# Seven tables of stops instead of one: numbers of their own for each body of a decoder-trunk kernel

## The chip, the cores and the metric

The kernel runs on one core of a Trainium2 chip. Its time is the device time of one execution in microseconds (us). Three runs of the kernel before took 3503.97, 3504.54 and 3508.67 us; the median, 3504.54 us, is the number to compare with.

## The reference, cut to what matters

One layer of a decoder trunk over a sequence of 1024 tokens of width 1024, all in f32: a mixer (latent attention with 4 heads, a gated recurrence, differential attention with 4 heads), a cross-attention over 256 memory rows, and a PEER feed-forward part that picks experts by product keys. A final norm follows.

```
q = (h @ w_q).reshape(b, s, PEER_HEADS, 2, PEER_DQ // 2)
sc = einsum('bshcd,cnd->bshcn', q, keys)
top_s, top_i = lax.top_k(sc, PEER_TOPK)            # 16 of 128, twice for each of 8 heads
cand = top_s[..., 0, :, None] + top_s[..., 1, None, :]
best_s, best_c = lax.top_k(cand, PEER_TOPK)        # 16 pairs for each head
act = gelu(einsum('td,thkd->thk', xt, u[et]))      # 128 experts for each token
y = einsum('thk,thkd->td', gt * act, v[et])
```

Every token has 8 x 16 = 128 experts, and for each it reads a row of u and a row of v, 1024 numbers each. For 128 tokens, one expert's rows are a tile of 128 x 1024 f32, 512 KB.

## The kernel before, in words

The sequence is cut into 8 blocks of 128 tokens. For each block the program has a front part (norms, projections, recurrence, attention, cross-attention, choice of experts: the "pieces" of the list `PIECES`) and an expert part of 128 positions. A position is one expert: GpSimd gathers its u tile and its v tile from memory (`gather_u`, `gather_v`), VectorE multiplies the u tile with the block's activations and sums along the row (L1986), ScalarE makes activations and a diagonal matrix from each coefficient (L1466), and TensorE multiplies the diagonal with the v tile and adds into PSUM (`add_row`, L1212). Of every eight v tiles one goes to VectorE instead (L2007).

The two parts are woven. Body b of the loops (b = 1 to 7; `LOOPS` has one body for each, since the attention of block b reads b + 1 key tiles) does the front part of block b between the 128 positions of block b - 1, and near its end some first pieces of block b + 1 (`next_norm`, `next_0` to `next_4`). Before the first body block 0's front part runs alone, and after the last body the positions of block 7 run alone.

How the two parts are woven is written in three lists of tables, `TENSOR_STOPS`, `VECTOR_STOPS` and `SCALAR_STOPS`, one table for each body. A table gives to each piece a row of stops. An engine that comes to the next step of a piece first does all its positions below the stop (`Pace.to`), and then the step. A step at stop 59 thus stands in the engine's program behind position 58 and ahead of position 59. Several steps with one stop follow each other with no position between them. The code that takes a stop is `Pace.part`, and the order of pieces, steps and positions among themselves is fixed; only where the two lists interleave is free.

What sets the order around it:
- Tiles of u and of v have a ring of 8 slots each (`G_RING`). GpSimd issues alternately the gather of u tile i and of v tile i - 12 (`retrieve`). The first waits until VectorE has used u tile i - 8 (`u_used`), the second until TensorE (or VectorE, for its share) has used v tile i - 20 (`v_used`, `v_added`). GpSimd is one queue in order: if either waits, both streams stop.
- On TensorE and ScalarE the v tile at position p is number p - 13 and the diagonal number p - 10 (`SUM_LAG`, `DIAG_LAG`), so that the engines are to be near the same position at any time.
- Weights come through a ring of 4 slots of two slices (`W_RING`), loaded by SyncE ahead as slots come free (`w_used`). SyncE has no stops. Behind the last `next` weights it waits for VectorE's copy at position 18 of the next body (`x_copied`, L1658) before it goes on.
- VectorE turns the end of the choice of experts into indices: `choose_0` hands the first half (`hand_first_ids`), which GpSimd needs before it gathers for the next block, and behind `choose_1` `hand_ids` hands the rest at the end of the body.

The pieces on which the prediction draws: `mla_0` to `mla_3` and `diff_0` to `diff_3` are the attention (on TensorE the scores L1061 and L1065, the transposes L1047 and the values L1073; on ScalarE the exponentials and the copies into pT, `out_pT`, L1252); `mix_out` and `cross_out` are the products L1127, `cross_q` and `peer_q` the products L979, as are the `next` pieces; `top_0` and `top_1` find 16 of 128 in eight rows each (L1869, L1873, L1875); `choose_0` and `choose_1` do the same for four rows each and then turn the places into numbers (two rounds of L1923, L1926, L1928 each, and small operations between).

## Time and profile before

| | us |
|---|---|
| median of three runs | 3504.54 |
| profiled execution, its own time | 3502.22 |
| span of that execution | 3500.1 |
| TensorE busy in the span | 2942.9 (84%) |
| VectorE busy | 2341.0 (67%) |
| GpSimd busy | 2008.2 (57%) |
| ScalarE busy | 814.6 (23%) |

The span runs from the first to the last instruction. Block 0's front part takes about the first 310 us, the seven bodies follow, and the positions of block 7 take the last 350 us. A row of a view names line, engine, operation and tiles; PE is TensorE, DVE VectorE, ACT ScalarE, POOL GpSimd.

### The profile page before, as it was taken

How to read it: one execution, taken by the hardware profiler on the slowest of the kernel's cores; microseconds unless marked ns; L12 is line 12 of the kernel's file. 1: busy time of each engine (PE TensorE's matmuls, PEld its weight loads, DVE VectorE, ACT ScalarE, POOL GpSimd, SP SyncE). 2: the span in 40 equal slices, each digit the busy share in tenths (PEclk: the TensorE clock that was granted, in tenths of full speed). 3: DMA queues.
4: the chain of work that ended last, by engine and by line, in shares of the span. 5: the costliest groups of instructions: out<-in, count | busy, mean ns of one | idle time of the engine just before them, and what ended most of it. 6: DMA issues, size and time to landing. Idle time of an engine off the chain costs nothing.

```text
span 3500.1 us, 34723 instructions
## 1 busy us (share of the span) xinstructions
PE 2942.9 (84%) x10960; PEld 1660.0 (47%) x10960; DVE 2341.0 (67%) x5884; ACT 814.6 (23%) x1924; POOL 2008.2 (57%) x2085
## 2 busy tenths in 40 slices
PE   7786898888997899888987799888998789976777
PEld 6465355533554355444554445544554445522222
DVE  6229756886578765887477855786648866596554
ACT  3111421133111422133211332114221232211111
POOL 1003765666565664666555655666547655577775
PEclk9897999999999999999999999999999999998999
DMA  7787999999999999999999999999999999999998
GB/s 275 259 299 266 409 409 409 408 409 402 409 402 408 399 405 403 407 409 390 405 409 408 397 351 409 409 408 370 354 409 409 409 346 350 390 404 410 409 409 339
DMA packets 387256, 1346.12 MB, mean 385 GB/s; under 512 B 41793, under 2 KB 44865, under 8 KB 386433
## 3 DMA queue, kind: packets, MB, share of 16 engines
q0 software_dynamic: 294912, 1073.87, 78.0%
q1 hardware_dynamic: 91008, 265.83, 20.1%
q10 hardware_dynamic: 1152, 4.19, 0.3%
q8 instruction: 89, 1.46, 0.2%
q14 instruction: 95, 0.77, 0.1%
HBM read 1334.03 MB, written 35.39 MB: 391 GB/s over the span
## 4 chain that ended last, share of the span: by engine, by line
PE 43%; DMA 25%; DVE 14%; POOL 9%; issue 6%; ACT 3%; SPq 0%; DVEq 0%; ACTq 0%; POOLq 0%
PE ps_sum L1212 19%; DMA rows<-in_peer_u,ids_u 9%; PE ps_p L979 7%; DMA rows<-in_peer_v,ids_v 6%; DMA rows<-in_peer_v,ids_u 5%; POOL rows L802 5%; PE ps_s L1127 5%; POOL rows L792 4%; DVE rows L1986 4%; DMA w_ring<-packed 2%; PE ps_s L1065 2%; PE ps_p L1073 2%; DVE feat_b L1873 1%; PE ps_p L1047 1%; DVE feat_b L1869 1%
## 5 line engine op out<-in xcount | busy, mean ns | idle before, releaser
L1212 PE MATMUL ps_sum<-rows,diag 128*128 128x512 f32 x3584 | 1748.0, 631 | 271.9 <-DMA rows<-in_peer_v,ids_v 129.2
L1986 DVE CUSTOM_DVE_ANT_0 rows<-h_cur,rows 128x1024 f32<-128x1024 f32 x1024 | 1228.1, 1220 | 539.7 <-DMA rows<-in_peer_u,ids_u 527.0
L792 POOL DMA_INDIRECT rows<-in_peer_u,ids_u x1024 | 1005.4, 982 | 720.7 <-issue 498.8
L1212 PEld LDWEIGHTS ps_sum<-rows,diag 128*128 128x128 f32 x3584 | 684.1, 201 | 1166.4 <-issue 1047.8
L802 POOL DMA_INDIRECT rows<-in_peer_v,ids_v x512 | 493.5, 964 | 452.2 <-PE ps_sum L1212 295.6
L802 POOL DMA_INDIRECT rows<-in_peer_v,ids_u x512 | 494.4, 966 | 267.8 <-issue 127.3
L1466 ACT ACTIVATE diag<-ident,acts 128x128 f32<-128x128 f32 x896 | 327.4, 394 | 1057.4 <-PE ps_sum L1212 757.5
L979 PE MATMUL ps_p<-hT,w_ring 128*128 128x128 f32 x2944 | 367.8, 286 | 36.1 <-DMA w_ring<-packed 18.0
L979 PEld LDWEIGHTS ps_p<-hT,w_ring 128*128 128x128 f32 x2944 | 362.0, 202 | 68.6 <-issue 42.3
L1772 DVE CUSTOM_DVE_ANT_0 e<-ps_s,bias_t 128x256 f32<-128x256 f32 (+6 forms) x96 | 74.2, 773 | 177.5 <-PE ps_s L1065 70.6
L2007 DVE SCALAR_TENSOR_TENSOR x_cur<-rows,acts,x_cur 128x1024 f32<-128x1024 f32 x128 | 164.0, 1282 | 13.4 <-DMA rows<-in_peer_v,ids_v 13.4
L1843 DVE TENSOR_TENSOR x_next<-x_next,ps_s 128x512 f32<-128x512 f32 x32 | 21.9, 685 | 189.8 <-PE ps_s L1127 189.8
L1454 ACT ACTIVATE acts<-dots 128x8 f32<-128x8 f32 x128 | 26.6, 207 | 453.2 <-DVE dots L1986 453.0
L1127 PE MATMUL ps_s<-w_ring,hT 128*128 128x512 f32 x256 | 117.7, 606 | 12.7 <-DVE hT L1833 6.8
L1379 ACT ACTIVATE e<-e,small 128x256 f32<-128x256 f32 (+6 forms) x96 | 75.4, 786 | 220.6 <-DVE small L1774 220.2
L979 PE MATMUL ps_p<-pT,w_ring 128*128 128x128 f32 x1024 | 118.6, 276 | 1.2 <-DMA w_ring<-packed 0.6
L979 PEld LDWEIGHTS ps_p<-pT,w_ring 128*128 128x128 f32 x1024 | 116.8, 192 | 5.6 <-issue 3.3
L1127 PE MATMUL ps_s<-w_ring,feat_b 128*128 128x512 f32 x256 | 115.4, 594 | 1.1 <-ACT feat_b L1252 0.7
L1065 PE MATMUL ps_s<-k_diff,feat_a 32*128 32x512 f32 (+2 forms) x192 | 84.2, 545 | 24.9 <-DVE small L1774 24.7
L1873 DVE FIND_INDEX8 feat_b<-feat_b,e 128x8 uint32<-128x128 f32 (+1 forms) x384 | 103.4, 279 | 0.0
L1252 ACT ACTIVATE feat_a<-ps_p 128x512 f32<-128x512 f32 (+2 forms) x48 | 26.0, 541 | 317.5 <-PE ps_p L979 317.4
L1986 DVE DVE_READ_ACCUMULATOR2_ANT dots<- 128x1 f32 x1024 | 84.5, 83 | 0.0
(280 smaller groups left out, 2325.7 us busy)
## 6 DMA issues: line engine op xcount, KB each, us to landing
w_ring<-packed SPq DMA_DIRECT2D x343, 512.0 KB, 7.7
w_ring<-in_wstream SPq DMA_DIRECT2D x65, 512.0 KB, 5.3
packed<-in_wstream SPq DMA_DIRECT2D x49, 512.0 KB, 7.9
rows<-in_peer_u,ids_u POOLq DMA_INDIRECT x1024, 13.3
rows<-in_peer_v,ids_u POOLq DMA_INDIRECT x512, 10.7
rows<-in_peer_v,ids_v POOLq DMA_INDIRECT x512, 15.4
bias_rows<-rows SPq DMA_DIRECT2D x5, 1024.0 KB, 12.8
bias_t<-in_x SPq DMA_DIRECT2D x8, 512.0 KB, 6.2
```

The source lines that it names most:

```text
L792: pool.indirect_dma_start(u_rows[:, j % G_RING, :], None, peer_u, bass.IndirectOffsetOnAxis(ap=ids_u[:, j:j + 1], axis=0)).then_inc(u_land ...
L802: pool.indirect_dma_start(v_rows[:, j % G_RING, :], None, peer_v, bass.IndirectOffsetOnAxis(ap=ids[:, j:j + 1], axis=0)).then_inc(v_landed ...
L979: ins = pe.matmul(dst, w[:, k, :], lhs[:, kt, :], start=(kt == 0), stop=(kt == KT - 1))
L1065: ins = pe.matmul(ps_s[:, c0:c1], q_diff[r:r + DK, half // 4, :], k_diff[r:r + DK, half // 4, c0:c1], start=True, stop=True)
L1127: pe.matmul(ps_s[:, n * 512:(n + 1) * 512], lhs[:, kt, :], w, start=(kt == 0), stop=(kt == KT - 1)).then_inc(w_used, 1)
L1212: ins = pe.matmul(ps_sum[:, c * 512:(c + 1) * 512], diag[:, n % 4, :], v_rows[:, j % G_RING, c * 512:(c + 1) * 512], start=(n == 0), stop= ...
L1379: act.activation(buf[:, 0:keys_n], buf[:, 0:keys_n], ACT.Exp, bias=small[:, 32 + n:33 + n], accum_out=small[:, 48 + n:49 + n]).then_inc(s_ ...
L1466: act.activation(diag[:, n % 4, :], ident[:, :], ACT.Copy, scale=coef[:, j:j + 1]).then_inc(diag_made, 1)
L1772: run(dve.tensor_tensor_reduce(buf[:, 0:keys_n], ps_s[:, 0:keys_n], bias[:, 0:keys_n], 1.0, -3.0e38, ALU.add, ALU.max, small[:, 16 + n:17 ...
L1873: dve.max_index(i[:, first:first + 8], v[:, first:first + 8], s).then_inc(top_step, 1)
L1986: dve.tensor_tensor_reduce(row, h_cur[:, :], row, 1.0, 0.0, ALU.mult, ALU.add, dots[:, p:p + 1]).then_inc(u_used, 1)
L2007: dve.scalar_tensor_tensor(x_cur[:, :], v_rows[:, j % G_RING, :], coef[:, j:j + 1], x_cur[:, :], ALU.mult, ALU.add)\
```

## The change

All numbers of the three lists are replaced. Before, the seven tables of each list are the same (the last lacks the `next` pieces). After, each body has its own. Nothing else in the program changes: the same instructions, in the same order within each piece, the same buffers, semaphores and transfers. A part of the diff, for the pieces named below (TensorE's body 5 and 7, VectorE's bodies 1, 5 and 7, ScalarE's body 7; a body's number counts from 1):

```diff
 TENSOR_STOPS, body 5
-"mla_0": (29, 30, 31), ... "diff_2": (45, 47, 48, 49), "diff_3": (49, 49, 51, 51), "join": (54, 56), "mix_out": (56, 56, 58, 58, 58),
+"mla_0": (29, 31, 32), ... "diff_2": (45, 47, 52, 52), "diff_3": (52, 52, 56, 56), "join": (56, 59), "mix_out": (59, 59, 60, 60, 60),
-"next_2": (112, 121, 121, 121, 121), "next_3": (121, 121, 124, 126, 126), "next_4": (126, 128, 128)
+"next_2": (108, 120, 120, 120, 120), "next_3": (120, 120, 120, 120, 120), "next_4": (120, 120, 120)
 TENSOR_STOPS, body 7
-"diff_2": (45, 47, 48, 49), "diff_3": (49, 49, 51, 51), "join": (54, 56), "mix_out": (56, 56, 58, 58, 58),
-"norm_cross": (59, 62), "cross_q": (62, 62, 62, 67, 67),
+"diff_2": (46, 51, 51, 52), "diff_3": (52, 52, 56, 56), "join": (56, 59), "mix_out": (59, 59, 59, 59, 59),
+"norm_cross": (59, 61), "cross_q": (61, 61, 61, 61, 61),
 VECTOR_STOPS, body 1
-"choose_0": (104, 105, 105, 105, 106, 108, 108, 108, 108, 111, 111), "top_1": (113, 113, 113, 113, 114, 117),
-"choose_1": (120, 120, 124, 125, 126, 126, 126, 128, 128, 128, 128)
+"choose_0": (107, 107, 107, 107, 107, 115, 115, 115, 115, 115, 115), "top_1": (115, 115, 115, 115, 123, 128),
+"choose_1": (128, 128, 128, 128, 128, 128, 128, 128, 128, 128, 128)
 VECTOR_STOPS, body 5
+"choose_0": (100, 100, 100, 100, 100, 104, 104, 104, 104, 121, 121), "top_1": (121, 121, 121, 121, 121, 121),
+"choose_1": (121, 121, 122, 123, 123, 123, 123, 123, 123, 123, 123)
 VECTOR_STOPS, body 7
-"top_0": (93, 94, 94, 94, 97, 99)
+"top_0": (95, 95, 95, 95, 95, 95), "choose_0": (95, 95, 95, 95, 104, 104, 104, 104, 104, 104, 104)
 SCALAR_STOPS, body 7
-"diff_0": (34, 38, 42), "diff_1": (42, 42, 42), "diff_2": (47, 47, 48), "diff_3": (48, 51, 53)
+"diff_0": (33, 38, 42), "diff_1": (42, 42, 42), "diff_2": (49, 49, 50), "diff_3": (50, 53, 53)
```

In words, for the rest: TensorE's attention runs from stop 29 (28 in body 3, 30 in body 6) to stop 51 in all bodies before; after, it ends at 52, 50, 52, 51, 56, 52 and 56 in bodies 1 to 7. VectorE's `top` and `choose` steps stand at fewer, larger stops in all bodies: `choose_1` wholly at 128 in body 1 and at 127 in body 2; in body 3 the last two steps of `choose_0`, all of `top_1` and seven steps of `choose_1` at 114; in body 4 the same with four steps of `choose_1`; in body 6 `top_1` at 109 and `choose_1` at 126. ScalarE's third stops of `diff_0` to `diff_3`, ahead of the copies into pT, are 42, 42, 48, 53 before in every body, and 41, 41, 50, 53 in body 5, 42, 42, 49, 49 in body 6 and 42, 42, 50, 53 in body 7 after. TensorE's stops ahead of the transposes that these copies follow are 40, 43, 48, 51 before, and 42, 45, 52, 56 in body 5, 41, 43, 48, 52 in body 6 and 40, 43, 51, 56 in body 7 after. TensorE's ten tiles of `next_2` to `next_4` stand at 116 in body 3 and at 120 in body 5.

## Rows read from the trace of the kernel before

**Rows 1.** The page: busy time of the engines, GB/s in 40 slices, the gathers' queue.

```profile
PE 2942.9 (84%) x10960; PEld 1660.0 (47%) x10960; DVE 2341.0 (67%) x5884; ACT 814.6 (23%) x1924; POOL 2008.2 (57%) x2085
...
GB/s 275 259 299 266 409 409 409 408 409 402 409 402 408 399 405 403 407 409 390 405 409 408 397 351 409 409 408 370 354 409 409 409 346 350 390 404 410 409 409 339
...
q0 software_dynamic: 294912, 1073.87, 78.0%
```

**Rows 2.** Busy time by stretches: attention, then mix_out, of bodies 5, 6, 7; `top_0`.

```profile
core 0: us, PE busy (x) PEld busy (x) DVE busy (x) ACT busy (x) POOL busy (x), PEclk, DMA share, GB/s
1980.00:2066.00 86.00, 75.81 (x275) 41.31 (x275) 57.00 (x118) 34.89 (x71) 49.91 (x51) 0.95 0.96 358
2066.00:2096.00 30.00, 28.83 (x72) 12.85 (x71) 13.99 (x37) 3.80 (x8) 12.95 (x14) 0.98 0.92 349
2393.00:2486.00 93.00, 82.03 (x301) 44.39 (x300) 59.78 (x119) 36.95 (x71) 51.52 (x52) 0.95 0.94 345
2486.00:2516.00 30.00, 29.15 (x73) 13.08 (x73) 13.72 (x38) 4.61 (x10) 13.57 (x15) 0.98 0.89 332
2815.00:2912.00 97.00, 84.10 (x322) 45.77 (x321) 60.60 (x115) 39.05 (x71) 48.92 (x50) 0.97 0.90 328
2912.00:2942.00 30.00, 29.15 (x72) 12.99 (x71) 14.36 (x39) 3.95 (x8) 13.09 (x14) 0.97 0.84 313
...
990.00:1000.00 10.00, 10.00 (x25) 4.45 (x24) 9.71 (x50) 2.00 (x6) 7.50 (x8) 1.00 0.96 358
...
3046.00:3066.00 20.00, 18.64 (x52) 9.61 (x51) 17.76 (x79) 5.83 (x12) 12.21 (x13) 1.00 0.88 321
```

**Rows 3.** Who GpSimd waited for in 2826 to 2942 us (total, times, longest).

```profile
POOL rows L802 <- PE ps_sum L1212: 29.4, 12, 5.9
POOL rows L792 <- DVE dots L1986: 15.0, 10, 8.0
```

**Rows 4.** Who TensorE waited for in body 7's attention, 2815 to 2912 us.

```profile
PE ps_p L1047 <- ACT pT L1252: 9.5, 8, 3.0
```

**Rows 5.** TensorE in order of time: start, us, group [idle before <-releaser].

```profile
2868.21 0.66 PE L1047 MATMUL ps_p<-ident,e 128*128 128x128 f32 x4 [0.69 <-ACT pT L1252]
...
2874.15 3.70 PE L1212 MATMUL ps_sum<-rows,diag 128*128 128x512 f32 x8
...
2286.24 7.31 PE L979 MATMUL ps_p<-hT,w_ring 128*128 128x128 f32 x64
```

**Rows 6.** Groups of instructions of the whole execution: busy us, mean ns | idle before.

```profile
L1986 DVE CUSTOM_DVE_ANT_0 rows<-h_cur,rows 128x1024 f32<-128x1024 f32 x1024 | 1228.1, 1220 | 539.7 <-DMA rows<-in_peer_u,ids_u 527.0 <-DVE e L1875 2.4 <-DVE small L1537 1.4
L1873 DVE FIND_INDEX8 feat_b<-feat_b,e 128x8 uint32<-128x128 f32 (+1 forms) x384 | 103.4, 279 | 0.0
...
L1869 DVE MAX8 feat_b<-e 128x8 f32<-128x128 f32 (+1 forms) x384 | 78.2, 273 | 3.5 <-ACT e L1252 1.1
L1875 DVE MATCH_REPLACE8 e<-feat_b,e 128x128 f32<-128x128 f32 (+1 forms) x192 | 51.9, 270 | 0.0
...
L1928 DVE TENSOR_REDUCE pT<-e 128x64 f32<-128x1024 f32 x32 | 39.0, 1219 | 0.9
L1873 DVE MATCH_VALUE_LOAD feat_b<-feat_b,e 128x8 f32 x384 | 30.2, 79 | 3.9 <-DVE feat_b L1869 0.5
...
L1875 DVE MATCH_VALUE_LOAD e<-feat_b,e 128x8 f32 x192 | 13.9, 72 | 0.1
...
L1950 DVE SCALAR_TENSOR_TENSOR h_cur<-x_next,small,ffn_row 128x1024 f32<-128x1024 f32 x8 | 10.3, 1285 | 0.0
...
L1914 DVE CAST pT<-pT 128x128 f32<-128x128 uint32 x16 | 3.9, 242 | 0.6
```

**Rows 7.** DMA issues of the whole execution: count, KB each, median us to landing.

```profile
w_ring<-packed SPq DMA_DIRECT2D x343, 512.0 KB, 7.7
...
rows<-in_peer_u,ids_u POOLq DMA_INDIRECT x1024, 13.3
```

**Rows 8.** TensorE's products with a weight slice, all blocks (the page's groups).

```profile
L1127 PE MATMUL ps_s<-w_ring,hT 128*128 128x512 f32 x256 | 117.7, 606 | 12.7 <-DVE hT L1833 6.8
```

More of the change, by code:

```diff
@@ L165 @@
 ]
 VECTOR_STOPS = [
-    {"latents": (0, 6), "mla_up": (8,), "conv": (17,), "gates": (19, 19, 21, 23), "recur": (25, 26), "mla_0": (26,),
-     "mla_1": (29,), "mla_2": (33,), "mla_3": (39,), "diff_0": (39, 39, 39), "diff_1": (42, 42, 43), "diff_2": (43, 45, 48),
-     "diff_3": (50, 52, 52), "join": (53, 54), "mix_out": (54, 55, 57, 57), "norm_cross": (59, 59, 63), "cross_scores": (71,),
-     "cross_mix": (71, 72), "cross_out": (73, 76, 84, 84), "norm_ffn": (85, 85, 85), "next_square": (90, 93),
[3 rows of a table removed]
@@ new lines @@
+    {"latents": (0, 5), "mla_up": (11,), "conv": (16,), "gates": (21, 21, 21, 23), "recur": (23, 26), "mla_0": (26,),
+     "mla_1": (29,), "mla_2": (35,), "mla_3": (39,), "diff_0": (39, 39, 39), "diff_1": (43, 43, 43), "diff_2": (43, 46, 49),
+     "diff_3": (49, 51, 51), "join": (52, 53), "mix_out": (53, 59, 59, 59), "norm_cross": (59, 59, 60),
+     "cross_scores": (72,), "cross_mix": (72, 72), "cross_out": (79, 79, 89, 89), "norm_ffn": (89, 89, 89),
+     "next_square": (89, 94), "top_0": (94, 94, 94, 94, 104, 105), "next_norm": (105, 105),
+     "choose_0": (105, 105, 105, 105, 105, 105, 105, 105, 105, 119, 119), "top_1": (123, 123, 123, 123, 123, 127),
+     "choose_1": (127, 127, 127, 127, 127, 127, 127, 127, 127, 127, 127)},
@@ new lines @@
+    {"latents": (0, 9), "mla_up": (9,), "conv": (17,), "gates": (21, 21, 22, 23), "recur": (23, 26), "mla_0": (26,),
+     "mla_1": (29,), "mla_2": (34,), "mla_3": (41,), "diff_0": (41, 41, 41), "diff_1": (42, 42, 43), "diff_2": (43, 46, 48),
+     "diff_3": (49, 52, 52), "join": (53, 54), "mix_out": (54, 57, 59, 59), "norm_cross": (59, 59, 69),
+     "cross_scores": (73,), "cross_mix": (73, 74), "cross_out": (77, 77, 77, 77), "norm_ffn": (77, 77, 77),
+     "next_square": (95, 95), "top_0": (95, 95, 95, 95, 105, 105), "next_norm": (105, 105),
+     "choose_0": (105, 105, 105, 105, 105, 105, 105, 105, 105, 114, 114), "top_1": (114, 114, 114, 114, 114, 114),
+     "choose_1": (114, 114, 114, 114, 128, 128, 128, 128, 128, 128, 128)},
@@ new lines @@
+    {"latents": (0, 3), "mla_up": (8,), "conv": (12,), "gates": (23, 23, 23, 23), "recur": (23, 26), "mla_0": (26,),
+     "mla_1": (30,), "mla_2": (34,), "mla_3": (39,), "diff_0": (39, 39, 39), "diff_1": (44, 44, 44), "diff_2": (44, 47, 49),
+     "diff_3": (52, 53, 53), "join": (55, 55), "mix_out": (55, 55, 61, 61), "norm_cross": (61, 61, 61),
+     "cross_scores": (75,), "cross_mix": (75, 75), "cross_out": (75, 75, 83, 83), "norm_ffn": (83, 83, 83),
+     "next_square": (83, 95), "top_0": (95, 95, 95, 95, 95, 95), "next_norm": (95, 101),
+     "choose_0": (101, 105, 105, 105, 105, 105, 105, 105, 105, 105, 105), "top_1": (109, 109, 109, 109, 109, 109),
+     "choose_1": (126, 126, 126, 126, 126, 126, 126, 126, 126, 126, 126)},
@@ new lines @@
+    {"latents": (2, 2), "mla_up": (5,), "conv": (18,), "gates": (19, 19, 23, 26), "recur": (26, 26), "mla_0": (26,),
+     "mla_1": (31,), "mla_2": (31,), "mla_3": (40,), "diff_0": (40, 40, 40), "diff_1": (44, 44, 44), "diff_2": (44, 52, 52),
+     "diff_3": (53, 53, 53), "join": (57, 57), "mix_out": (57, 57, 59, 59), "norm_cross": (59, 59, 74),
+     "cross_scores": (74,), "cross_mix": (74, 74), "cross_out": (74, 74, 80, 80), "norm_ffn": (80, 80, 80),
+     "top_0": (95, 95, 95, 95, 95, 95), "choose_0": (95, 95, 95, 95, 104, 104, 104, 104, 104, 104, 104),
+     "top_1": (114, 114, 114, 114, 114, 114), "choose_1": (114, 114, 126, 126, 126, 126, 126, 126, 126, 126, 126)},
```

169 lines of the change are left out of this document (81 added, 88 removed), and 53 rows, old and new, of tables (SCALAR_STOPS, VECTOR_STOPS).

## The prediction

> **What bounds the kernel now.** I read the page first. The GB/s line [rows 1] has one ceiling: 409 GB/s, held in most slices from the fifth on, so the gathers set the pace almost everywhere. They move 1073.87 MB in 2048 transfers, 524 KB each, which at 409 GB/s is 1.28 us: a position (one u and one v tile) costs 2.56 us of transfer. No edit of the stops changes a byte. What it can change is the time in which less than 409 GB/s moves. I call (409 - GB/s)/409 x length the lost time of a stretch. The slices below 409 are in the last third and the busy times by stretches [rows 2] say where: attention loses 10.7 us in body 5 (358 GB/s over 86 us), 14.6 us in body 6 and 19.2 us in body 7, the 30 us behind it, with `mix_out`, 4.4, 5.6 and 7.0 us. That is 61.5 us. `top_0` loses 1.2 us in body 2 (358 GB/s over 10 us; body 3 repeats it) and 4.3 us in body 7 (321 over 20 us). Bodies 1 to 4 are otherwise near the ceiling. So some 70 us lie open, 2% of the time.
>
> Why transfers are missing there: GpSimd waits 29.4 us for TensorE's row sums and 15.0 us for VectorE's rows between 2826 and 2942 us [rows 3]. TensorE is busy 84.10 of 97 us in body 7's attention, and 29.15 of 30 behind it [rows 2]. A row of its sum is four matmul records, 1.85 us [rows 5], for seven of eight positions, thus 1.62 us a position. Against 2.56 us of transfer that leaves it 0.94 us a position for the front part. Attention asks for much more, TensorE falls behind, and once it is about seven positions behind, the 8 slots of v are full and the gathers stop.
>
> The Trainium skill ("Perfetto Trace Analysis", section "Identifying the Most-Contended Engine") says that matmul busy time misjudges TensorE's headroom and that the weight loads' share is to be used. That share is 45.77 of 97 us here [rows 2], half empty, and by it TensorE isn't what binds, giving attention more positions brings nothing, and the sum below ends 9.4 us higher, which is the third rival. Rows 3 speak against it, since the queue waits for TensorE by name.
>
> **The change part by part.** Only stops move, so nothing is added or removed; each part shifts work along the positions.
>
> *Attention over more positions (bodies 5 and 7).* Its last stop on TensorE goes from 51 to 56. Five more positions lie beside the same front work: 5 x 0.94 = 4.7 us less lag in each, -9.4 us. Bodies 1 to 4 and 6 move by one or two positions; that is worth nothing I can tell. The bounds are -9.4 and 0: 0 where the lag only moves to what follows.
>
> *mix_out and cross_q in one piece each (body 7).* `mix_out` now stands wholly at 59, `cross_q` wholly at 61. `mix_out` is 117.7/8 = 14.7 us of TensorE [rows 8] beside 8 weight transfers, 8 x 1.28 = 10.2 us; `cross_q` is 8 tiles, a quarter of 7.31 us each [rows 5], 14.6 us beside 10.2. Together 8.9 us of lag at two positions' distance, where before it was split at 56, 58, 62 and 67. TensorE comes there at the end of its slack; positions 56 to 61 give 5 x 0.94 = 4.7 back. I take +3 us (bounds 0 and 8.9 - 4.7 = +4.2).
>
> *The waits of TensorE inside attention.* It waits 9.5 us in body 7 for ScalarE's copies into pT [rows 4]. Eight waits of 0.69 us [rows 5] are within a transpose pair and stay, 5.5 us. The other 4.0 come where ScalarE's stop lies behind TensorE's, as before 53 against 51 in `diff_3` and 42 against 40 in `diff_0`. After, ScalarE comes first in `diff_1` to `diff_3` of bodies 5 and 7 and in all but `diff_0` and `diff_2` of body 6. TensorE being late, each us saved there is one. The idle time of the three stretches is 10.2, 11.0 and 12.9 us [rows 2], less 5.5 each: 17.6 us in all that stops can reach. I take two thirds, -12 us; bounds -17.6 and +6 (new stops can make new waits, a third as large).
>
> *VectorE's large blocks of `top` and `choose`.* A row on VectorE is 1.22 us [rows 6]. The work: the finds are 78.2 + 103.4 + 30.2 + 51.9 + 13.9 = 277.6 us over 8 blocks, 34.7 a block; a `top` is a third, 11.6, a `choose` a sixth, 5.8. A `choose` adds six passes of 1.22 us (7.3) and a dozen small operations like the 0.24 us one, about 3; `choose_1` some 2 more for the gates; so `choose_0` is 16.1, `choose_1` 18.1, and `hand_ids` adds 1.5 (1.29 of it L1950) [rows 6]. While VectorE does such a block, no u slot comes free. What the DMA engines can still do is at most the 8 pairs of the rings, 8 x 2.56 = 20.5 us, and the weights that TensorE asks for meanwhile. A gap longer than that stops them:
> - body 1, at 128: last find of `top_1` 2.8, `choose_1` 18.1, hand-over 1.5, next row 1.2 = 23.6, and the weight queue is empty or blocked. +3.1 us.
> - body 2, at 127: 2.8 + 18.1 + 1.2 = 22.1. +1.6 us.
> - body 3, at 111 and 114: 13.5, then 2.9 + 11.6 + 11.7, with three rows (1.4 us with their share of v) and the next one: 45. Against 11 pairs (28.2) and at most 12 weight transfers (15.4), 43.6. +1.4 us.
> - body 4, at 114: 2.9 + 11.6 + 6 + 1.2 = 21.7, and some lag left from a block of 21 us at 105. +3 us.
> - body 5, at 121 to 123: 2.9 + 11.6 + 18.1, two rows and the next, 36.6, against 10 pairs (25.6) and 6 weights (7.7), 33.3. +3.3 us.
> - body 6, at 126: 19.3 fits; body 7, at 95: 11.6 + 6 + 1.2 = 18.8 fits only if TensorE isn't late, as before (I leave the 4.3 us).
>
> Sum +12.4. The old 1.2 us of `top_0` in bodies 2 and 3 go, since weights aren't missing at the new place: -2.4. Net +10 us. Bounds: 0 if the weights always fill in, and from the median of 13.3 us from issue to landing [rows 7], which says that the rings usually hold 10 transfers and not 16, up to 7.7 us more in each of five blocks: +10 + 5 x 4 (half of that, as the blocks of 3 and 5 are met by weights) = +30.
>
> The Trainium skill ("DMA: Bandwidth & Descriptors", section "Anatomy of one DMA — SWDGE (gpsimd) path") gives each such transfer about 2 us of fixed cost beside its bytes. By it every stop of the queue costs 2 us more before a row lands, an estimate of +10 us for five blocks, and the sum would turn positive. No row here shows an emptied queue starting again; it would add to the first rival.
>
> Sum: -9.4 + 3 - 12 + 10 = -8.4 us. The profiled execution took 3502.22 us (span 3500.1), so its like is 3493.8; the median of the runs lies 2.3 us above it, and the forecast is **3496 us**.
>
> **The rivals.**
> *VectorE's blocks decide (slower).* The mechanism is the one above at its upper bound: rings hold less than 8 pairs when a block begins, because TensorE holds v slots at the same time (its ten `next` tiles stand in one piece at 116 to 124, 18.3 us). For it: no old block comes near 20 us, so no row shows that it is hidden, and the rings' usual content is 13.3 us. Against: weights fill in just there. Price +30, waits in attention not recovered (0) and attention -9.4 + 3: +24, 3528; at half the bounds +14, 3518. From a net price above 18 us it outweighs the rest.
> *Attention's waits go entirely and the blocks cost nothing.* -9.4 + 0 - 17.6 - 2.4 - 4.3 = -34: 3471.
> *The lag only moves.* TensorE is busy without a pause from the start of attention to `cross_q` (29.15 of 30 us), so the same work meets the same transfers whatever the stops, and VectorE's blocks stay under the weights: between -3 and +3, 3504. For it: all of the 0.94 us a position is lent and paid back within 15 positions.
>
> **How the numbers follow.** The forecast's case 0.40 (own range 3486 to 3506, two thirds of it faster by over 7 us); slower by the blocks 0.32; all waits gone 0.15; lag moves 0.13. 0.2% is 7 us, about what three runs can tell. Faster: 0.27 + 0.15 = 0.42. Same: 0.13 + 0.13 = 0.26. Slower 0.32. The range goes from the far gain to near the upper slow case: 3471 to 3523.
>
> **What would show it.** GB/s over attention of bodies 5 to 7 rises only a little (358, 345, 328 before), TensorE's waits for pT fall towards 5.5 us a body. VectorE shows gaps of 20 us between rows at 128, 127, 114 and 121, and GB/s dips behind them for a few us. The forecast is wrong if those dips are 5 us and more each, or if attention still loses 61 us in all and nothing else appears; and if attention loses under 30 us, the gain is several times mine.

## The result, and the profile after

The changed kernel takes **3621.2 us** (median of 5 runs, 3617.5 to 3624.1), the kernel before 3504.5 us beside it (3500.2 to 3509.8): ratio 1.0335, 95% interval 1.0317 to 1.0354. It is 117 us slower. The forecast was 3496 us, the range 3471 to 3523: wrong in direction and size.

The page after, the three lines that answer to [rows 1]:

```profile
PE 2980.3 (82%) x10960; PEld 1682.3 (46%) x10960; DVE 2340.0 (65%) x5884; ACT 820.4 (23%) x1924; POOL 2004.6 (55%) x2085
...
GB/s 283 257 266 333 392 398 396 390 391 392 378 374 366 400 385 396 403 404 345 389 405 400 384 305 392 379 400 358 331 396 388 393 328 339 378 396 398 410 409 350
...
q0 software_dynamic: 294912, 1073.87, 76.3%
```

The instructions and the bytes are the same. TensorE's busy time is 37 us longer for them, at a mean granted clock of 0.928 against 0.940. What is gone is the ceiling: before, 20 of the 36 slices from the fifth on stood at 407 to 410 GB/s, now two do. Cutting the trace at the first u row of each body gives a body a row. Before, bodies 1 to 7 (columns: stretch, its length, busy time and count of PE, PEld, DVE, ACT, POOL, then granted clock, DMA share, GB/s):

```profile
316.00:704.00 388.00, 328.40 (x1229) 188.20 (x1230) 274.43 (x708) 91.44 (x229) 241.49 (x252) 0.91 1.01 397
704.00:1105.00 401.00, 346.46 (x1293) 193.81 (x1293) 284.27 (x724) 97.26 (x238) 249.04 (x257) 0.94 1.02 406
1105.00:1508.00 403.00, 351.46 (x1316) 198.07 (x1316) 286.65 (x723) 99.27 (x238) 247.08 (x257) 0.95 1.02 405
1508.00:1911.00 403.00, 351.36 (x1366) 202.31 (x1366) 288.73 (x725) 102.29 (x238) 251.54 (x257) 0.97 1.02 404
1911.00:2323.00 412.00, 359.50 (x1389) 205.57 (x1388) 290.38 (x724) 104.42 (x238) 250.26 (x257) 0.96 1.01 394
2323.00:2743.00 420.00, 367.49 (x1412) 209.92 (x1412) 292.61 (x723) 106.41 (x238) 249.59 (x256) 0.96 1.00 389
2743.00:3153.00 410.00, 347.59 (x1168) 180.96 (x1168) 291.09 (x711) 105.27 (x230) 248.53 (x256) 0.96 0.97 378
```

After, the same seven:

```profile
315.00:717.00 402.00, 328.93 (x1224) 188.57 (x1224) 274.19 (x707) 92.88 (x229) 239.76 (x251) 0.91 1.00 392
717.00:1143.00 426.00, 355.94 (x1302) 202.90 (x1303) 284.42 (x724) 99.53 (x239) 245.95 (x252) 0.92 0.97 375
1143.00:1552.00 409.00, 349.65 (x1308) 195.54 (x1306) 286.50 (x724) 99.67 (x238) 251.16 (x259) 0.95 1.01 397
1552.00:1976.00 424.00, 367.98 (x1372) 209.54 (x1373) 287.71 (x723) 102.79 (x238) 249.45 (x259) 0.93 1.00 387
1976.00:2413.00 437.00, 369.31 (x1383) 210.40 (x1381) 290.57 (x725) 104.97 (x238) 245.86 (x253) 0.92 0.96 372
2413.00:2846.00 433.00, 371.22 (x1411) 213.17 (x1412) 292.31 (x723) 106.15 (x237) 244.89 (x252) 0.93 0.97 373
2846.00:3274.00 428.00, 357.99 (x1171) 187.50 (x1170) 291.64 (x712) 106.47 (x231) 256.66 (x264) 0.93 0.96 364
```

With the prediction's formula, (409 - GB/s)/409 x length, the bodies lose 90 us before and 212 us after. The difference, 122 us, is the whole result (the two profiled executions differ by 119). Body 2 alone goes from 2.9 to 35.4 us, bodies 1 to 4 from 23 to 87. Those were the bodies that the prediction left "otherwise near the ceiling".

The attention and mix_out stretches of bodies 5 to 7, the counterpart of [rows 2]:

```profile
2045.00:2154.00 109.00, 94.37 (x299) 48.81 (x298) 64.70 (x133) 38.84 (x78) 60.48 (x64) 0.89 0.86 321
2154.00:2184.00 30.00, 26.98 (x62) 11.86 (x61) 12.06 (x31) 2.43 (x6) 11.37 (x12) 0.89 0.93 344
2483.00:2590.00 107.00, 94.03 (x316) 49.13 (x316) 65.35 (x140) 38.14 (x73) 60.43 (x63) 0.90 0.86 319
2590.00:2620.00 30.00, 27.47 (x94) 14.51 (x95) 14.13 (x32) 2.63 (x7) 11.50 (x13) 1.00 0.98 373
2911.00:3030.00 119.00, 103.92 (x338) 53.19 (x337) 73.51 (x145) 41.16 (x74) 67.59 (x69) 0.90 0.89 328
3030.00:3060.00 30.00, 28.32 (x83) 14.79 (x84) 11.36 (x38) 4.81 (x13) 8.89 (x11) 0.89 0.83 280
```

They lose 23.5 + 4.8 + 23.5 + 2.6 + 23.6 + 9.5 = 87.5 us, where [rows 2] gave 61.5. The idle time of TensorE in the three attention stretches went up, from 34.1 to 14.6 + 13.0 + 15.1 = 42.7 us; the stretches themselves are 335 us long instead of 276, so its share is the same, 12 to 13%. The granted clock in them is 0.89 to 0.90, before it was 0.95 to 0.97.

**What a dip looks like.** Body 7's attention after. VectorE in order of time (start, us, engine, line, operation, [idle before <-releaser]), then the busy times of 10 us of the gap:

```profile
2941.06 1.23 DVE L1772 CUSTOM_DVE_ANT_0 e<-ps_s,bias_t 128x1024 f32<-128x1024 f32 x1 [1.57 <-PE ps_s L1061]
2942.21 0.08 DVE L1772 DVE_READ_ACCUMULATOR2_ANT small<- 128x1 f32 x1
2942.33 0.15 DVE L1774 TENSOR_SCALAR small<-small 128x1 f32<-128x1 f32 x1
2953.26 1.23 DVE L1772 CUSTOM_DVE_ANT_0 e<-ps_s,bias_t 128x1024 f32<-128x1024 f32 x1 [10.78 <-PE ps_s L1061]
```

```profile
2945.00:2955.00 10.00, 10.00 (x34) 5.97 (x33) 1.68 (x4) 1.17 (x3) 1.40 (x2) 0.73 0.68 247
```

VectorE's `mla_1` and `mla_2` both stand at 31 in this table (29 and 33 before). The second needs scores which TensorE makes only after ScalarE's exponentials of the first, the transposes and the values. So VectorE does one step, waits 10.8 us, does the next, and no row of its own stands between. Its u slots stay full, GpSimd is busy 1.40 of 10 us, and 247 GB/s move. The wait would have been there before too; but then VectorE had four rows to do in it. The chain also runs slowly: TensorE has just stood for 3.0 us, and its one row in the gap takes 3.6 us at a granted clock of 0.50, against 1.9 us at full clock (2940 to 2949 us of its trace).

The largest dip in attention is TensorE's own. In body 5 three steps of `mla_3` and two of `diff_0` stand at stop 35 in its table (35, 35, 37 and 37, 38 before). From 2074.0 to 2087.9 us it does no row, the granted clock is 0.50 from 2080 to 2090, GpSimd waits for it, and 15 us lose 12.7:

```profile
POOL rows L802 <- PE ps_sum L1212: 15.0, 1, 15.0
...
2080.00:2095.00 15.00, 13.62 (x23) 6.09 (x23) 2.94 (x7) 2.21 (x7) 2.40 (x3) 0.55 0.21 63
```

The wait can also lie across two tables, as around the end of body 2: who waited for whom between 1110 and 1160 us (total, times, longest), and 10 us of it:

```profile
PE ps_sum L1212 <- ACT diag L1466: 11.0, 1, 11.0
ACT pT L1433 <- DVE pT L1907: 10.3, 1, 10.3
```

```profile
1130.00:1140.00 10.00, 10.00 (x19) 4.31 (x20) 9.52 (x15) 2.79 (x6) 3.77 (x4) 0.78 0.30 93
```

ScalarE's `choose_1` stands at 120, but the step of VectorE's `choose_1` that makes its operand (L1907) at 127. VectorE is in its block of `choose_1` and does no row; ScalarE stands at 120 for it, its diagonals stop, TensorE stands for them, and no v slot comes free either. Until 1130 the transfers already under way still make 395 to 409 GB/s; the 10 us shown lie behind the wait. TensorE begins again at 1129.9, at a granted clock of 0.50 until 1134, GpSimd's next gather begins only at 1135.3, and over these 10 us 93 GB/s move.

**Two conditions.** The runs fell under two conditions: in three groups (the pair above is one) the kernel before took 3503 to 3505 us, in three others 3716 to 3734 us, and there the changed kernel's ratio is larger (1.085). Ratios are therefore compared within one condition, called **A** (3504) and **B** (3716 to 3734); one chip showed both at different times. What the traces of B show is in the last section. One execution, of ten of `before_spread`, took 4180 us at a granted clock of 0.67 and is in no ratio.

### The profile page after: what moved, and what is told of

Same layout as the page of the kernel before. It is cut to its first block, busy times and chain, and to the rows that moved or that the text cites. A ratio compares the mean times of both kernels' runs of the same rounds, so it can differ in the third digit from the quotient of the medians.

```text
span 3619.4 us, 34703 instructions
## 1 busy us (share of the span) xinstructions
PE 2980.3 (82%) x10960; PEld 1682.3 (46%) x10960; DVE 2340.0 (65%) x5884; ACT 820.4 (23%) x1924; POOL 2004.6 (55%) x2085
## 4 chain that ended last, share of the span: by engine, by line
PE 43%; DVE 20%; DMA 20%; POOL 7%; issue 5%; ACT 4%; SPq 0%; DVEq 0%; ACTq 0%; POOLq 0%
PE ps_sum L1212 21%; DMA rows<-in_peer_u,ids_u 9%; PE ps_p L979 6%; DVE rows L1986 6%; PE ps_s L1127 5%; DMA w_ring<-packed 5%; POOL rows L802 4%; POOL rows L792 3%; DMA rows<-in_peer_v,ids_u 3%; DMA rows<-in_peer_v,ids_v 2%; PE ps_s L1065 2%; DVE feat_b L1873 2%; PE ps_p L1073 2%; DVE feat_b L1869 1%; DVE e L1875 1%
## 5 line engine op out<-in xcount | busy, mean ns | idle before, releaser
L1212 PE MATMUL ps_sum<-rows,diag 128*128 128x512 f32 x3584 | 1721.4, 629 | 281.4 <-ACT diag L1466 104.5
L1212 PEld LDWEIGHTS ps_sum<-rows,diag 128*128 128x128 f32 x3584 | 693.1, 201 | 1201.9 <-issue 1003.1
L979 PE MATMUL ps_p<-hT,w_ring 128*128 128x128 f32 x2944 | 360.5, 284 | 42.5 <-DMA w_ring<-packed 35.3
L979 PEld LDWEIGHTS ps_p<-hT,w_ring 128*128 128x128 f32 x2944 | 352.2, 199 | 63.2 <-issue 27.5
L1252 ACT ACTIVATE pT<-ps_p 128x512 f32<-128x512 f32 (+2 forms) x112 | 52.2, 471 | 165.4 <-PE ps_p L1047 143.5
L1127 PEld LDWEIGHTS ps_s<-w_ring,hT 128*128 128x128 f32 x256 | 48.9, 199 | 81.9 <-issue 51.8
## 6 DMA issues: line engine op xcount, KB each, us to landing
bias_rows<-rows SPq DMA_DIRECT2D x5, 1024.0 KB, 12.3
```

The lines of the kernel that those rows point to most:

```text
L979: ins = pe.matmul(dst, w[:, k, :], lhs[:, kt, :], start=(kt == 0), stop=(kt == KT - 1))
L1127: pe.matmul(ps_s[:, n * 512:(n + 1) * 512], lhs[:, kt, :], w, start=(kt == 0), stop=(kt == KT - 1)).then_inc(w_used, 1)
L1212: ins = pe.matmul(ps_sum[:, c * 512:(c + 1) * 512], diag[:, n % 4, :], v_rows[:, j % G_RING, c * 512:(c + 1) * 512], start=(n == 0), stop= ...
```

## The experiments

All kernels differ from one of the two by numbers in the three lists alone. Either all three lists of a body or section are exchanged, or numbers are moved within what the neighbouring steps allow. Every run's ratio is to the kernel before under the same condition. The first theory after the result was **coupling**: a step before the stop of its producer on another engine holds the rows behind it, as ScalarE's `choose_1` above. Its rival was **blocks**: much work of one engine at one stop, whoever waits.

**1. `rep_all`, B.** The changed kernel with all such stops raised to the producer's:

```diff
 SCALAR_STOPS, body 2 (others alike)
-"cross_scores": (67,), ... "choose_1": (120, 120)
+"cross_scores": (72,), ... "choose_1": (122, 127)
```

> The changed kernel, with one thing put right in it: wherever a step on one engine stood at an earlier stop than the step of another engine that makes its operand, it stands at that producer's stop (4 to 13 pieces a body move, in all three tables; no block of steps is split, several become larger). Coupling theory (the 117 us come from engines that reach a waiting step too early and hold their own rows behind it): most of the loss goes, the time is 3520 to 3570 us, and the waits of TensorE's latents for VectorE (13.4 us) and of ScalarE's choose_1 (10.3 us) in body 2 fall under 4 us. Block theory (blocks of steps longer than the eight slots of the row ring hold the rows, whoever waits for whom): the blocks are as large or larger, so 3610 to 3640 us.

Measured 4036.0 us against 3731.5: 1.0824 (1.0787 to 1.0861); the changed kernel under the same condition, run 5, 1.0847 (1.0799 to 1.0895). The intervals overlap: nothing came back that can be told, and coupling, put so, fell in B. But the edit also gathers steps that stood apart (in body 2 TensorE's last step of `mix_out`, both of `norm_cross` and three of `cross_q` now stand together at 59), so it changes two things at once. In sum TensorE's blocks did not grow: stretches of over 10 us of its work without a row have 587 us here and 631 in the changed kernel, both traces of B.

**2 to 4. `b14_new`, `blk_128`, `tail_old`, B.** Bodies 5 to 7 as before; VectorE's `choose_1` of the kernel before wholly at 128; everything from `peer_q` on as before:

```diff
 VECTOR_STOPS, all bodies (blk_128)
-"choose_1": (120, 120, 124, 125, 126, 126, 126, 128, 128, 128, 128)
+"choose_1": (128, 128, 128, 128, 128, 128, 128, 128, 128, 128, 128)
```

> The changed kernel with the numbers of before in bodies 5, 6 and 7: only bodies 1 to 4 have their new numbers. By the lost transfer time of the two traces (before 3.1, 3.4, 4.7, 5.3 us in bodies 1 to 4; after 9.9, 35.7, 11.8, 22.8 us), the losses are of each body's own making and add: 3504 + 64 = about 3568 us. If instead a body's loss is carried to the next ones (an engine that starts a body late), bodies 5 to 7 lose more than in the kernel before and it is over 3580 us; if the loss sits in the attention of bodies 5 to 7 alone, 3504 to 3515 us.

> The kernel before with one edit: VectorE's choose_1 (eleven pieces, which stand at stops 120 to 128) stands wholly at stop 128 in all seven bodies, one block before the next body; ScalarE's choose_1 stays at 125, TensorE's latents at 1. The block alone was put at +3 us a body at most. Block theory: +2 to +3 us a body, 3515 to 3525 us. Coupling theory: ScalarE reaches choose_1 three positions before VectorE has made its operand and TensorE its latents one position after the block, both hold rows behind them; 5 to 8 us a body over six bodies, 3535 to 3555 us.

> The changed kernel with the second part of each body as before: from peer_q on (on VectorE from next_square on) all three tables have the numbers of the kernel before, in all bodies; where an older number would stand before its neighbour's new one it is raised to it (norm_ffn at 89 in body 3, for one). The new numbers stay from latents to norm_ffn. By the dips in the trace of after about half of the extra lost time lies from stop 85 on and at the body's start behind the blocks at its end (9.2 + 8.1 us around body 2's two ends): coupling theory and block theory both say 3550 to 3575 us, and what is left is the loss of the first part (cross attention and the three attention blocks). If the first part carries all, 3610 us or more.

Measured 1.0454 (1.0404 to 1.0504), 1.0028 (1.0002 to 1.0053) and 1.0643 (1.0604 to 1.0682). The losses are spread over the bodies: four of seven bodies give 0.045 of 0.085. One block of some 20 us of VectorE a body costs 10 us in all. With the second half of the body old, three quarters of the loss stay.

**5 to 8. `after_again`, `front_new`, `att_new`, `cross_new`, B.** The changed kernel unedited, and the kernel before with one section of all tables new.

> The changed kernel, nothing edited, as the yardstick of this group of runs. In the first group of runs the kernel before took 3731 us, and its variants 1.003 (block at 128) to 1.082 times as long, so the chip and not only the kernel sets the loss. If this chip is as the first pair of traces, 3621 us, ratio 1.033; if it is as that of the first group of runs, about 1.08 times the kernel before: bodies 1 to 4 alone gave 1.045, and seven bodies would be 7/4 of it.

> The kernel before with the new numbers of the changed kernel for the steps latents, mla_up, conv, gates and recur alone (stops 0 to 29), in all three tables and all seven bodies. Coupling theory: TensorE's latents stands 2 to 7 positions before VectorE's in bodies 1 and 7 and ScalarE's mla_up 3 to 4 before TensorE's in bodies 4 to 6, so a quarter of the loss of after_again. Throughput theory (the new numbers pack TensorE's work into the attention and cross stretches more densely than rows can be fed beside it): next to nothing, under a tenth of that loss.

> The kernel before with the new numbers for mla_0 to diff_3 and join alone (stops 26 to 59) in all tables and bodies. The prediction put this part at -9.4 us, since bodies 5 and 7 have more positions for the same attention. Coupling theory: the new numbers give no waits between engines longer than those of the kernel before here (V.join against T.join 3 to 4 positions in bodies 1, 3 and 4), so -10 to +10 us. Block theory (several attention pieces of TensorE share one stop, for example four at 31 and three at 37): a third to a half of the loss of after_again.

> The kernel before with the new numbers for mix_out, norm_cross, cross_q, cross_scores, cross_mix, cross_out and norm_ffn alone (stops 52 to 89) in all tables and bodies. Coupling theory: here the mismatches are most (ScalarE's cross_scores five positions before VectorE's in body 2, TensorE's mix_out three before VectorE's, ScalarE's cross_mix three before TensorE's in bodies 5 to 7): a third to a half of the loss of after_again, most of it in bodies 2 and 4. Block theory: cross_q and cross_out in one or two pieces (8.5 and 8.9 us of TensorE's weight products at one stop) give about as much, spread evenly over the bodies.

| kernel, condition B | ratio | interval |
|---|---|---|
| after_again | 1.0847 | 1.0799 to 1.0895 |
| front_new (latents to recur) | 1.0074 | 1.0048 to 1.0101 |
| att_new (attention, join) | 1.0185 | 1.0152 to 1.0217 |
| cross_new (mix_out to norm_ffn) | 1.0355 | 1.0315 to 1.0395 |

The three sections add up to 0.061, `tail_old` with all three has 0.064, and the rest to 0.085 is the tail's 0.020. So in B the loss is made locally, section by section, and the prediction's section with a gain, attention, costs 1.9%.

**9 to 12. `after_spread`, `pe_lump`, `v_lump`, `before_spread`, A.** Over the nine kernels of B the loss went with the time of TensorE's blocks. So TensorE's pieces were spread in the changed kernel and in the kernel before, and made into blocks in the kernel before; and VectorE's made into blocks.

```diff
 TENSOR_STOPS, body 2 (after_spread)
-"mix_out": (55, 55, 55, 55, 55), ... "cross_q": (57, 57, 57, 65, 65), ... "cross_out": (73, 73, 73, 82, 82)
+"mix_out": (53, 53, 54, 55, 56), ... "cross_q": (57, 58, 59, 63, 64), ... "cross_out": (73, 74, 75, 81, 82)
 VECTOR_STOPS, all bodies (v_lump)
-"top_0": (93, 94, 94, 94, 97, 99), "choose_0": (104, 105, 105, 105, 106, 108, 108, 108, 108, 111, 111),
-"top_1": (113, 113, 113, 113, 114, 117), "choose_1": (120, 120, 124, 125, 126, 126, 126, 128, 128, 128, 128)
+"top_0": (93, 99, 99, 99, 99, 99), "choose_0": (104, 108, ...), "top_1": (117, ...), "choose_1": (128, ...)
```

> The changed kernel with TensorE's table alone edited: where many of its pieces share a stop they are spread over the neighbouring stops, as far as the tables of VectorE and ScalarE (untouched, with all their large blocks) allow without a longer wait. TensorE-block theory (TensorE's work between two rows is what costs: over the nine kernels run so far the loss goes with the microseconds of TensorE's blocks over 7 us, about 1 us for 1 us, and not with VectorE's): most of the loss over the kernel before goes, from +8.5% to +1 to +3.5%. VectorE-block theory: VectorE's 25 blocks over 10 us are unchanged, +6 to +8%. Coupling theory: the waits between lists are unchanged, +6 to +8%.

> The kernel before with TensorE's table alone edited, the other way round: mix_out wholly at stop 58, cross_q at 63, cross_out at 78, peer_q at 85, next_0 and next_1 at 107, in all bodies; each of these blocks is 7 to 9 us of products between two rows, and no engine waits for another more than one position longer than before. TensorE-block theory: 13 to 15 us more a body over a bound of 5 us at 0.9 us each, +80 to +110 us, ratio 1.02 to 1.03. Coupling and VectorE-block theory: 0 to +20 us.

> The kernel before with VectorE's table alone edited: top_0 in one block at 99, choose_0 in one at 108, top_1 in one at 117, choose_1 in one at 128, in all bodies; together about as much VectorE work in blocks over 10 us as in the changed kernel. TensorE-block theory: +10 to +25 us (the block at 128 alone gave 0.3%). VectorE-block theory (the prediction's second rival): the eight slots of the row ring run full behind each block, +80 us or more.

> The kernel before with TensorE's pieces spread by the same rule, VectorE's and ScalarE's tables untouched: no stop of TensorE has more than about 2.5 us of work, where before several had 4 to 6.5 us (mix_out's last three parts at 58, next_2's four at 121). TensorE-block theory: faster than the kernel before by 10 to 60 us. Other theories: no difference, within 0.3%.

| kernel, condition A | ratio | interval | us against before |
|---|---|---|---|
| changed kernel | 1.0335 | 1.0317 to 1.0354 | +117 |
| after_spread | 1.0312 | 1.0292 to 1.0332 | +109 |
| pe_lump | 1.0051 | 1.0035 to 1.0067 | +18 |
| v_lump | 1.0091 | 1.0070 to 1.0112 | +32 |
| before_spread | 1.0018 | 1.0006 to 1.0030 | +6 |

The theory of TensorE's blocks fell here: about 8 us come back, which the intervals don't tell from nothing, five large blocks a body cost 18 us, and spreading them in the kernel before brings no gain. VectorE's four blocks a body cost 32 us. How a single one is borne is seen in `v_lump` around stop 128 of body 2, where two rows of VectorE begin 20.4 us apart:

```profile
1095.00:1115.00 20.00, 9.93 (x49) 6.30 (x47) 18.21 (x57) 4.64 (x9) 6.60 (x7) 0.88 1.03 408
1115.00:1130.00 15.00, 15.00 (x33) 7.05 (x33) 14.55 (x34) 2.49 (x6) 8.66 (x9) 0.82 0.95 357
```

The rings carry 408 GB/s through these 20 us, and 52/409 of 15 us, 1.9 us, are lost behind it. In the changed kernel two rows are 20.3 us apart around the block at 127, with ScalarE held at 120, and 258 GB/s move over 25 us:

```profile
1120.00:1145.00 25.00, 15.12 (x30) 6.66 (x31) 23.38 (x80) 4.95 (x12) 8.59 (x10) 0.80 0.71 258
```

That is 9.2 us. The other engines aren't idle bystanders in `v_lump` either: TensorE waits 2.4 us for a diagonal and 7.7 us for VectorE. But ScalarE finds its operand made and goes on in the middle of the block, TensorE does a row, and GpSimd's two waits of 4.4 and 7.8 us have a gather between them; in the changed kernel GpSimd issues nothing for 14.0 us, and for 5.0 us no gather's packet moves. The pair shows that the longer stop of the gathers costs more; that ScalarE's stop alone makes it is the reading of the waits, not of an edit.

TensorE's clock is a rival that no edit sets apart. It stands at half of full speed for 425 us of the kernel before and 521 us of the changed one. But the time at half clock doesn't go with the loss: 530 us in `v_lump` (+32 us) and 369 us in `pe_lump` (+18 us).

**13 to 15. `after_vspread`, `rep_tspread`, `all_fix`, A.** From the changed kernel: VectorE's pieces spread (attention kept); consumers raised to their producers and TensorE spread, so that no block grows; both, with a position to spare where the neighbours allow it.

```diff
 body 2 (all_fix)
-VECTOR "top_0": (94, 94, 94, 94, 104, 105), "choose_0": (105, 105, 105, 105, 105, 105, 105, 105, 105, 119, 119)
+VECTOR "top_0": (94, 95, 95, 97, 102, 104), "choose_0": (108, 109, 110, 111, 112, 113, 113, 114, 114, 115, 115)
-SCALAR "cross_scores": (67,), ... "choose_1": (120, 120)
+SCALAR "cross_scores": (72,), ... "choose_1": (122, 127)
-TENSOR "cross_q": (57, 57, 57, 65, 65)
+TENSOR "cross_q": (60, 60, 60, 63, 65)
```

> The changed kernel with VectorE's table alone edited: where many of its pieces share a stop they are spread over neighbouring stops (its attention pieces stay), between the stops that TensorE's and ScalarE's untouched tables allow. VectorE-block theory (the row ring and the engines behind VectorE run dry while it works through a block; in the last group of runs four such blocks a body in the kernel before cost 32 us, and spreading TensorE's pieces in the changed kernel brought back under 10 us of 117): where the kernel before takes about 3504 us the ratio falls from 1.0335 to 1.012 to 1.022. If the blocks of VectorE are without weight and the waits between the tables are all: 1.028 to 1.036. Where the kernel before takes about 3730 us (changed kernel 1.085), 1.05 to 1.07 and 1.08 to 1.09.

> The changed kernel with every step at or after the stop of its producer on another engine (as in the run with all of these put right), and TensorE's pieces then spread (its attention pieces stay), so that putting right the one thing doesn't make TensorE's blocks longer, as it did there. VectorE's blocks stay. Coupling theory: with a kernel before of 3504 us, 1.005 to 1.018; with one of 3730 us, 1.02 to 1.05. VectorE-block theory: 1.025 to 1.035, or 1.07 to 1.085.

> Both at once: the changed kernel with its waits between tables put right with a position to spare where the neighbours allow it, and the pieces of VectorE and of TensorE spread; attention pieces and the general places of the steps stay as in the changed kernel. If blocks and waits together are the whole loss: within 0.5% of the kernel before, or below it, on either chip. If it is the places themselves (each step's distance to the work of the DMA and to the rows) that cost: still 1.5% or more above it.

Measured 1.0251 (1.0234 to 1.0268), 1.0245 (1.0225 to 1.0265) and 1.0139 (1.0122 to 1.0156). Against the changed kernel's 1.0335 that is 29, 32 and 69 us given back (x 3504 us): the two edits are worth about the same and add, with 8 us over. 48 us stay. The trace of `all_fix` says where. Cut at VectorE's rows, positions 24 to 63 (attention, with mix_out and cross_q) lose 71 us over the seven bodies before, 115 in the changed kernel and 111 in `all_fix`; all other positions 19, 95 and 27 us. So the edits gave back nearly all that lay outside positions 24 to 63, and 40 of the 47 us that `all_fix` loses more than the kernel before lie inside them. Its positions 24 to 63 of bodies 5, 6, 7, then positions 64 to 23 of the next body behind bodies 5 and 6:

```profile
1999.00:2143.00 144.00, 126.24 (x380) 62.92 (x379) 84.23 (x185) 43.44 (x90) 77.94 (x82) 0.91 0.89 334
2418.00:2568.00 150.00, 132.59 (x434) 68.63 (x433) 92.18 (x203) 46.30 (x90) 81.97 (x84) 0.91 0.90 337
2846.00:3001.00 155.00, 134.80 (x462) 69.83 (x461) 92.33 (x192) 48.11 (x91) 78.98 (x84) 0.92 0.88 327
2143.00:2418.00 275.00, 238.34 (x1005) 142.66 (x1004) 201.25 (x534) 60.35 (x149) 165.66 (x169) 0.96 1.03 408
2568.00:2846.00 278.00, 243.38 (x983) 146.23 (x982) 199.58 (x523) 62.30 (x150) 168.03 (x173) 0.95 1.02 407
```

Outside attention the ceiling is back (408 and 407). In attention next to nothing is: 84 us lost in the three stretches. The same positions before and after, bodies 5 to 7:

```profile
1973.00:2108.00 135.00, 122.76 (x442) 66.83 (x443) 85.99 (x191) 43.74 (x91) 75.70 (x79) 0.96 0.96 364
2386.00:2527.00 141.00, 128.10 (x466) 69.40 (x466) 88.28 (x193) 45.80 (x91) 77.28 (x80) 0.96 0.94 350
2808.00:2954.00 146.00, 131.70 (x490) 71.50 (x491) 89.91 (x191) 47.54 (x90) 74.78 (x79) 0.98 0.90 336
```

```profile
2046.00:2188.00 142.00, 124.34 (x384) 63.39 (x383) 77.78 (x164) 41.43 (x86) 72.87 (x77) 0.89 0.87 328
2486.00:2622.00 136.00, 121.98 (x425) 64.80 (x425) 80.73 (x170) 40.72 (x79) 71.23 (x74) 0.92 0.89 330
2911.00:3067.00 156.00, 138.73 (x473) 74.01 (x473) 91.87 (x190) 46.92 (x87) 79.98 (x82) 0.90 0.88 323
```

61 us before, 87 after; bodies 1 to 4 lose 10 us there before, 28 after and 27 in `all_fix`. `all_fix` had kept the attention stops, VectorE's pair at 31 and TensorE's five steps at 35 in body 5 among them, and the dip at 35 is there again, 15 us at 73 GB/s:

```profile
2040.00:2055.00 15.00, 13.62 (x24) 6.01 (x24) 3.00 (x7) 2.21 (x6) 2.46 (x3) 0.54 0.24 73
```

That one place loses 12.3 us; no edit moved it alone.

**16 to 18. `all_fix_attold`, `att_57`, `stretch`, B.** `all_fix` with attention as before; the kernel before with new attention in bodies 5 and 7 only; the kernel before with attention of bodies 5 to 7 over two more positions, all lists moved alike.

```diff
 body 5, 6, 7 (stretch): stops 13 to 34 one less, 47 to 91 one more, in all three lists
-TENSOR "mla_0": (29, 30, 31), ... "diff_3": (49, 49, 51, 51)
+TENSOR "mla_0": (28, 29, 30), ... "diff_3": (50, 50, 52, 52)
```

> The last kernel (changed kernel with waits put right and blocks spread, 1.0139 where the kernel before took 3503 us) and, besides, join and all attention pieces (mla_0 to diff_3) at their stops of before in all three tables. In its trace the lost transfer time that is left beyond that of the kernel before lies at positions 24 to 63 (+40 us), in attention. If that is the cause: ratio 0.998 to 1.004 (at 3730 us for the kernel before: under 1.015). If attention isn't it and the loss comes from the places of the other steps: 1.008 or more.

> The kernel before with the new attention stops (mla_0 to diff_3, join; mix_out pushed behind them) in bodies 5 and 7 alone, the two whose last attention stop goes from 51 to 56. By the prediction's first term these two bodies save 4.7 us each: -9.4 us, ratio 0.997. If what counts is how the pieces lie inside the stretch (TensorE has four pieces at 52 and two at 56 in body 5, three at 35, and the two tables behind it other stops): 0 to +15 us, ratio 1.000 to 1.004.

> The kernel before with attention of bodies 5 to 7 over two more positions and nothing else: in all three tables alike, stops 13 to 34 come one earlier, 47 to 91 one later, so that no step changes its place against a step of another engine or against its neighbour by more than one, and no block grows. If the lack of positions is what costs in attention (lost transfer time 15, 21 and 32 us in these bodies), two positions of 0.94 us each give 3 x 1.9 = 5.6 us: -4 to -8 us, ratio 0.998. If the lag only moves to what follows: 0.

Measured 1.0135 (1.0085 to 1.0185), 1.0083 (1.0057 to 1.0110) and 1.0087 (1.0060 to 1.0114). Of the 8.5% of condition B five sixths are given back with blocks and waits put right and attention old. How much of that is attention's isn't known, since `all_fix` itself wasn't run in B. The prediction's first term alone, new attention in bodies 5 and 7, costs 0.8% where it was to give 0.3%. And `stretch`, which gives attention two positions and takes one from the steps on either side of it, costs as much: more positions for attention are no gain in B. Whether they are in A wasn't run; `all_fix` with old attention wasn't run there either, so the 48 us are placed in positions 24 to 63 by the trace alone.

None of the kernels beats the kernel before.

## Why the prediction was wrong

*What bounds the kernel* was right: 409 GB/s is the ceiling, the bytes are the same, and the lost time of the stretches accounts for the result (122 us, for 117 of the medians and 119 of the profiled executions). The time that lies open was 90 us, not 70: bodies 1 to 4 lose 23 us before, half of it in body 1, and the prediction counted 1.2 us in each of two bodies. The error lies in what makes lost time.

*Attention over more positions, -9.4 us (bounds -9.4 and 0): wrong in sign.* The step treated TensorE's lag as a balance, so much work against 0.94 us a position, as if the work could be done at any time in the stretch. After, the stretches lose 26 us more, not 9.4 less. At positions 48 to 55 the three bodies did lose less (by the transfer records 9 us, 25 before), which is the part of the term that was right; but 24 to 31 lose 13 us more than before, 40 to 47 lose 15 us more and 56 to 63 lose 18 us more, over all bodies. There the steps are a chain, scores on TensorE, maximum on VectorE, exponential on ScalarE, transposes, values, and next scores. In a chain it counts how many rows stand between two steps of the same engine; with none, as at VectorE's 31 and TensorE's 35, the engine frees no slot for as long as the chain takes.

*TensorE's waits inside attention, -12 us (bounds -17.6 and +6): wrong in sign.* It was looked for whether ScalarE's stop lies ahead of TensorE's in each `diff`, and not how far each table's own steps lie apart. The wait that the term names, TensorE's for ScalarE's copies, fell by 2.5 us in the three bodies (25.7 to 23.2), but others grew: in body 7 TensorE waits 5.1 us for VectorE ahead of the scores (1.6 before), and 5.0 us go to v rows that haven't landed. Idle time rose by 8.6 us, in longer stretches. And "new stops can make new waits" was bounded for these three stretches only. **This is the step that failed**: the same question was asked for no other piece. In the tables it could have been read: in body 2 ScalarE's `choose_1` at 120 against VectorE's 127, `cross_scores` 67 against 72, TensorE's `mix_out` 55 against 59. Putting such stops right, with TensorE spread, was worth 32 us; TensorE's spreading alone gave about 8, which is no more than noise.

*VectorE's large blocks, +10 us (bounds 0 and +30): mechanism right, size at the upper end.* 29 us come back with them spread, 32 us are lost with four of them in the kernel before. A single block in `v_lump` comes near what was worked out: the rings held for 20 us and 1.9 us are lost behind it. [rows 7]'s ten transfers did not limit it, for GpSimd goes on issuing into free slots during the block, seven gathers in these 20 us. What was missing is that the blocks were summed for five places, where the trace has 21 stretches of over 10 us of VectorE's work without a row (none before), and that at some of them another engine waits.

*mix_out and cross_q in one piece, +3 us:* not measured by itself; five such blocks in every body cost 18 us (`pe_lump`), 0.5 us each.

*The rivals.* "VectorE's blocks decide" had the right direction and a fifth of the price, 24 of 117 us. "The lag only moves" and "waits go entirely" are refuted. The Trainium skill's rule on the weight loads' share ("Perfetto Trace Analysis", section "Identifying the Most-Contended Engine"), by which more positions bring nothing, came nearer than the term it spoke against, though the queue does wait for TensorE. The Trainium skill's fixed cost of a transfer ("DMA: Bandwidth & Descriptors", section "Anatomy of one DMA — SWDGE (gpsimd) path"), by which a stopped queue costs some 2 us beyond its gap, is neither shown nor refuted. The trace after does show an emptied queue starting again, in body 2: the last packet ends at 1132.4, GpSimd's next gather begins at 1135.32 and takes 1.42 us, and its first packet moves at 1137.4, 2.1 us behind the beginning of the issue and 0.7 us behind its end. What such a restart costs in all was not worked out.

My own first theory after the result, coupling alone, failed too (`rep_all`), and so did the second, TensorE's blocks, although it fitted nine kernels of condition B. Shares as they stand, of 117 us in A: VectorE's blocks 29, stops ahead of their producers with TensorE's blocks 32, 8 more when both are put right together, attention and what else is left 48. The first three are shown by edits; the last is placed by the trace, and which of its stops cost what is open.

## What to carry to other kernels

A balance of work against room says what a stretch can hold, not whether it will: in a program woven by hand, also list for each step its producer on the other engine, and for each engine the rows between two steps of one chain, and price every pair that comes out at zero or below. A block on one engine is borne by the rings up to their content (here about 20 us), as long as the engines beside it still free some slots. And an explanation that fits nine runs of one condition by a regression should be tried by an edit of the suspected cause alone before it is believed.
